# A decoder layer on one core: split products in cross-attention's output projection, bias rows in the upper part of A

## The reference, cut to what matters

```
def memory_cross_attention(hn, memn, w_xq, w_xkv, w_xo):
    ...
    s = jnp.einsum('bshd,bmhd->bhsm', q, k) * XATTN_HEAD_DIM ** -0.5
    p = jax.nn.softmax(s, axis=-1)
    o = jnp.einsum('bhsm,bmhd->bshd', p, v).reshape(B, S, D)
    return o @ w_xo                      # 256x1024 by 1024x1024

def moe_ffn(...):
    logits = xt @ w_router + b_router
    ...
    gu = xb @ w_gate_up[e] + b_gate_up[e]     # w_gate_up: 32 x 1024 x 2048
    ...
    return hmid @ w_down[e] + b_down[e]       # w_down: 32 x 1024 x 1024
```

## Time and profile before

| | us |
|---|---|
| median of 3 runs (1182.55 to 1183.7) | 1182.78 |
| the profiled execution | 1183.28 |
| its span | 1181.5 |
| PE busy | 1114.9 (94%) |
| DVE busy | 320.5 (27%) |
| ACT busy | 233.0 (20%) |
| POOL busy | 41.1 (3%) |

### The profile page before, as it was taken

How to read it: one execution, slowest core, us unless ns; L and a number is a source line. 1 busy time by engine, 2 the same in 40 slices (tenths; PEclk the granted TensorE clock), 3 DMA queues, 4 the chain that set the end, 5 groups by cost and what they waited for, 6 DMA issues and landing times.

```text
span 1181.5 us, 12743 instructions
## 1 busy us (share of the span) xinstructions
PE 1114.9 (94%) x5408; PEld 495.3 (42%) x5409; DVE 320.5 (27%) x719; ACT 233.0 (20%) x460; POOL 41.1 (3%) x41
## 2 busy tenths in 40 slices
PE   8999999999999999799999999999999999999896
PEld 7887668753333333233333333333333333333332
DVE  5787665332111112111222111111111111111112
ACT  6575665431000001000100000000000000000002
POOL 0010240220000000000000000000000000000000
PEclk9999999999999999899999999999999999999999
DMA  9915337779999999999999999999999999999995
GB/s 361 350 52 178 108 143 285 262 293 423 429 427 427 428 429 426 426 429 427 427 427 429 428 425 429 428 426 428 429 426 428 429 427 427 428 428 428 426 429 227
DMA packets 44586, 445.50 MB, mean 377 GB/s; under 512 B 6096, under 2 KB 10288, under 8 KB 19728
## 3 DMA queue, kind: packets, MB, share of 16 engines
q1 hardware_dynamic: 42784, 444.38, 90.3%
q10 hardware_dynamic: 1744, 0.28, 0.2%
HBM read 443.60 MB, written 1.05 MB: 376 GB/s over the span
## 4 chain that ended last, share of the span: by engine, by line
PE 65%; DMA 28%; DVE 4%; ACT 2%; issue 1%; SPq 0%; DVEq 0%; ACTq 0%
PE ps L2087 23%; PE ps L2096 13%; DMA R<-in_w_gate_up 12%; PE ps L1590 4%; DMA R<-in_w_down 4%; DMA XMT<-in_w_gate_up 4%; DMA MK<-in_w_gate_up 4%; PE ps L2116 4%; DMA A<-in_w_gate_up 4%; PE ps L2063 4%; PE ps L1610 3%; PE ps L1612 3%; PE ps L1611 3%; PE ps L1947 2%; PE ps L2078 2%; PE ps L1839 1%
## 5 line engine op out<-in xcount | busy, mean ns | idle before, releaser
L2087 PE MATMUL ps<-R,convT 128*64 128x512 f32 x1104 | 246.2, 593 | 14.3 <-DMA R<-in_w_gate_up 14.3
L1488 DVE TENSOR_SCALAR A<-ps 128x512 f32<-128x512 f32 x30 | 20.7, 692 | 645.8 <-PE ps L2087 645.8
L2087 PEld LDWEIGHTS ps<-R,convT 128*64 128x64 f32 x1104 | 76.8, 137 | 169.9 <-issue 137.2
L2096 PE MATMUL ps<-R,A 128*64 128x512 f32 x592 | 131.9, 593 | 1.3 <-DMA R<-in_w_down 1.2
L956 ACT ACTIVATE A<-A 128x512 f32<-128x512 f32 x30 | 18.9, 630 | 471.7 <-DVE A L1488 471.7
L2096 PEld LDWEIGHTS ps<-R,A 128*64 128x64 f32 x592 | 41.4, 137 | 78.8 <-issue 75.1
L2116 PE MATMUL ps<-A,convT 64*128 64x512 f32 x248 | 61.6, 615 | 2.1 <-ACT A L963 1.4
L963 ACT COPY A<-ps 128x512 f32<-128x512 f32 x30 | 17.6, 585 | 221.3 <-PE ps L2096 221.3
L2063 PE MATMUL ps<-H,convT 128*64 128x512 f32 x256 | 60.4, 592 | 0.1
L2078 PE MATMUL ps<-A,convT 96*64 96x512 bf16 x192 | 33.0, 393 | 20.6 <-ACT A L961 13.7
L2087 PE MATMUL ps<-XMT,convT 128*64 128x512 f32 x208 | 46.9, 593 | 2.0 <-DMA XMT<-in_w_gate_up 2.0
(11 more groups left out here) (323 smaller groups left out, 1287.9 us busy)
## 6 DMA issues: line engine op xcount, KB each, us to landing
R<-in_w_gate_up SPq DMA_DIRECT2D x69, 2048.0 KB, 35.3
R<-in_w_down SPq DMA_DIRECT2D x37, 2048.0 KB, 39.7
...
```

Of the source, the lines that this page charges most:

```text
L1488: V.tensor_scalar(gcl, bank(G_BANK), LIM, None, ALU.min).then_inc(m_gcl, 1)
L2087: last = mm(bank(b)[s * SLOTS:(s + 1) * SLOTS, :], xg[:, 4 * (j % 2) + 2 * c + j // 2, :], w[:, c * 2 * FF + at + s * BANK:c * 2 * FF + at ...
L2096: last = mm(bank(o)[s * SLOTS:(s + 1) * SLOTS, :], h[:, c, i * SLOTS:(i + 1) * SLOTS], w[:, c * D + s * BANK:c * D + (s + 1) * BANK], star ...
```

## The change

The output projection is made of split products. Its units are 16 more of the same kind (`UNITS_O`): raw weights in R as before, low parts in their place, high parts in tile QK, eight at a time, so that the second eight wait for the block (1,0) that last reads the first eight. The output's own high and low parts take XMT (`o_hi`, `o_lo`). The blocks' order becomes first half of (0,0), transposes, rest of (0,0), then (1,0), (0,1), (1,1), with the router's transposes inside (1,1). QK and A change places in the ring: fill 4 goes to A, fill 7 to QK. Fill 4 has no wait of its own any more, 6 waits for block (1,0), 7 for the last block, 8 and 9 for nothing more. The raw biases stand in A's columns 5632 to 7680 and in convT, and POOL alone splits them (`bias_parts`), at once when they land. The router's rows move from XMT to A's upper part (`h2T`), where they wait for the biases (`pool_bias`). Two counters of POOL become one (`pool_mix`).

```diff
--- before.py
+++ after.py
@@ -194,6 +196,8 @@
             return (R_p if base is R else A_p)[:, at:at + BANK]
 
         def high(u):
+            if u >= UNITS_O:
+                return QK_p[:, u % KC * BANK:(u % KC + 1) * BANK]
             if u >= UNITS:
                 at = (12288, 4096)[u // KC - 7] + u % KC * BANK
                 return R_p[:, at:at + BANK]
...
+        o_hi = XMT_p[:, 2048:4096].rearrange("p (t c n) -> p t c n", t=T, c=KC)
+        o_lo = XMT_p[:, 0:2048].rearrange("p (t c n) -> p t c n", t=T, c=KC)
         h_hi = XMT_p[:, 0:2048].rearrange("p (k n) -> p k n", k=KC)
         h_lo = XMT_p[:, 2048:4096].rearrange("p (k n) -> p k n", k=KC)
         sq_junk = [QK[:, 2048 + t * D:2048 + (t + 1) * D] for t in range(T)]
         P2T = xtf.rearrange("p (t h m n) -> p t h m n", t=T, h=XH, m=2)
 
         R_slot = [R[:, f * 4096:(f + 1) * 4096] for f in range(6)]
...
+        ring = [R_slot[0], R_slot[2], R_slot[1], R_slot[3], A[:, 0:4096], XM[:, :], R_slot[4], QK[:, :], R_slot[5], XMT[:, :],
                 MK[:, MOE_KEEP:MOE_KEEP + 4096]]
 
 
         BW = 2 * FF + D
-        b_raw = A[0:96, 0:BW]
+        b_raw = [A[0:96, 5632:5632 + 2 * FF], convT[0:96].rearrange("p c n -> p (c n)")]
         b_prt = A[0:96, 4096:4096 + BW // 2].bitcast(BF16)
         gcl, ucl, sgm, hmf, orow = (A[:, 5632 + 512 * i:6144 + 512 * i] for i in range(5))
         hTm = hmf.rearrange("p (c n) -> p c n", c=4)
         hT_b, selT_b, orow_b = sgm.rearrange("p (c n) -> p c n", c=4), gcl[:, 0:S], hmf
         junk = [A[:, 6144:7168], A[:, 6144:7168]]
+        h2T = A[:, 5632:7680].rearrange("p (k n) -> p k n", k=KC)
+        h2_junk = A[:, 7680:8192].bitcast(BF16)
         early_junk = convT[:].rearrange("p c n -> p (c n)")
 
         cvf = convT[:].rearrange("p c n -> p (c n)")
...
@@ -514,21 +521,15 @@
                             sp.wait_ge(g_done, 1)
                     if n == 2:
                         sp.wait_ge(pe_two, TWO["q", 1])
-                        for part in range(3):
-                            sp.dma_start(b_raw[part * E:(part + 1) * E, 0:2 * FF], b_gate_up[0]).then_inc(ld_bias, 16)
-                            sp.dma_start(b_raw[part * E:(part + 1) * E, 2 * FF:BW], b_down[0]).then_inc(ld_bias, 16)
-                    if n == 4:
-                        sp.wait_ge(pe_s2, T)
+                        for i, src in enumerate((b_gate_up, b_down)):
+                            for part in range(3):
+                                sp.dma_start(b_raw[i][part * E:(part + 1) * E, :], src[0]).then_inc(ld_bias[i], 16)
                     if n == 5:
                         sp.wait_ge(pe_two, TWO["oT", 1])
                     if n == 6:
+                        sp.wait_ge(pe_unit, UNITS + KC)
+                    if n == 7:
                         sp.wait_ge(pe_xo, 3)
-                    if n == 7:
-                        sp.wait_ge(act_part, 3)
-                    if n == 8:
-                        sp.wait_ge(pe_xo, 4)
-                    if n == 9:
-                        sp.wait_ge(pe_lg, T)
                     if n == 10:
                         sp.wait_ge(pe_cnt, T + 1)
                         sp.wait_ge(m_bsel, 1)
...
@@ -594,11 +595,18 @@
                     pool.wait_ge(act_osq, t + 1)
                     fold_squares(sq[:, t:t + 1])
 
-                def bias_rest(n):
-                    pool.wait_ge(act_part, 3 - n)
-                    link(nc.gpsimd.tensor_tensor(b_raw[0:n * E], b_raw[0:n * E], b_prt[0:n * E], ALU.subtract), pool_res)
-
-                bias_rest(2)
+                def bias_parts(i):
+
+                    raw = b_raw[i]
+                    prt = b_prt[:, 2 * FF * i:2 * FF * i + raw.shape[1]]
+                    pool.wait_ge(ld_bias[i], 16 * 3)
+                    link(nc.gpsimd.tensor_copy(prt, raw))
+                    for n in (2, 1):
+                        link(nc.gpsimd.tensor_tensor(raw[0:n * E], raw[0:n * E], prt[0:n * E], ALU.subtract))
+                        link(nc.gpsimd.tensor_copy(prt[0:n * E], raw[0:n * E]), pool_bias)
+
+                bias_parts(0)
+                bias_parts(1)
                 pool.wait_ge(pe_two, TWO["pv", 1])
                 link(nc.gpsimd.iota(iot.rearrange("p (s n) -> p s n", s=2), pattern=[[0, 2], [1, SLOTS]], base=0,
                                     channel_multiplier=0, allow_small_or_imprecise_dtypes=True), pool_moe)
...
+                    else:
+                        act.wait_ge(ld_o2, 32)
+                        act.wait_ge(pe_s2, T)
                     if 4 <= u < UNITS:
                         act.wait_ge(pe_unit, slot_free(u))
-                    if u >= UNITS:
+                    if u >= UNITS_O + KC:
+                        act.wait_ge(pe_unit, UNITS + kc + 1)
+                    if UNITS <= u < UNITS_O:
                         nc.scalar.activation(high(u), raw(u), ACT.Copy, scale=prm[:, R_XA + kc:R_XA + kc + 1]).then_inc(act_uhi, 1)
                     else:
                         nc.scalar.copy(high(u), raw(u)).then_inc(act_uhi, 1)
...
                 exps2(1)
                 pv_second(0)
                 second("pT", 1, 5, P2T[:, 1, 2:4].rearrange("p h m n -> p (h m n)"))
-                second("oT", 0, 1, last_half(oT2, 0))
-                act.wait_ge(ld_bias, 16 * 6)
-                nc.scalar.copy(b_prt, b_raw).then_inc(act_part, 1)
+                split_high("oT", 0, o_hi[:, 0])
+                for u in range(UNITS_O + 4, UNITS_O + 6):
+                    unit_high(u)
                 pv_second(1)
-                second("oT", 1, 5, last_half(oT2, 1))
-                for n in (2, 1):
-                    act.wait_ge(pool_res, 3 - n)
-                    nc.scalar.copy(b_prt[0:n * E], b_raw[0:n * E]).then_inc(act_part, 1)
+                for u in range(UNITS_O + 6, UNITS_O + 8):
+                    unit_high(u)
+                split_high("oT", 1, o_hi[:, 1])
+                for u in range(UNITS_O + 8, UNITS_O + 16):
+                    unit_high(u)
+                act.wait_ge(pool_bias, 4)
                 for t in range(T):
-                    act.wait_ge(dve_h2, 2 * t + 2)
-                    act.wait_ge(pe_two, TWO["oT", t])
-                    root(t, H[:, t, :], junk[t]).then_inc(act_rt, 1)
+                    act.wait_ge(dve_h2, 3 + t)
+                    root(t, H[:, t, :], h2_junk).then_inc(act_rt, 1)
                     if t == 0:
                         second_gain("h2T", t, R_MOE)
                 for t in range(T):
...
 
                 first("pT", 0, 0, P2T[:, 0, 0:2].rearrange("p h m n -> p (h m n)"))
                 max2(1)
+                for u in range(UNITS_O, UNITS_O + 3):
+                    unit_low(u)
                 pv_first(0)
                 first("pT", 1, 4, P2T[:, 1, 0:2].rearrange("p h m n -> p (h m n)"))
-                first("oT", 0, 0, first_half(oT2, 0))
+                unit_low(UNITS_O + 3)
+                split_low("oT", 0, o_hi[:, 0], o_lo[:, 0])
                 pv_first(1)
-                first("oT", 1, 4, first_half(oT2, 1))
+                for u in range(UNITS_O + 4, UNITS_O + 6):
+                    unit_low(u)
+                split_low("oT", 1, o_hi[:, 1], o_lo[:, 1])
+                for u in range(UNITS_O + 6, UNITS_O + 8):
...
+                        dve.wait_ge(pe_unit, UNITS + KC)
+                    else:
+                        dve.wait_ge(pe_xo, 1 + t + n)
                     hn = H[:, t, n * BANK:(n + 1) * BANK]
                     link(V.tensor_tensor(hn, hn, bank(4 * t + 2 + n), ALU.add), dve_h2)
 
@@ -1942,16 +1973,17 @@
                                         high(u), low(u), c)
                     return last
 
-                def half_rows(t, n, lhs, w, chunks=range(KC)):
+                def half_rows(t, n, chunks=range(KC)):
                     for c in chunks:
-                        last = mm(bank(4 * t + 2 + n), lhs(c), w(c, n), start=(c == 0), stop=(c == KC - 1))
+                        u = UNITS_O + n * KC + c
+                        if c % 4 == 0:
+                            pe.wait_ge(dve_sp, SPLIT["oT", t] + c // 4 + 1)
+                        if t == 0:
+                            pe.wait_ge(dve_ulo, u + 1)
+                        last = split_mm(bank(4 * t + 2 + n), o_hi[:, t, c, :], o_lo[:, t, c, :], high(u), low(u), c)
+                        if (t, n) == (1, 0):
+                            last.then_inc(pe_unit, 1)
                     return last
-
-                def wo(c, n):
-                    return w_o2[:, n, c, :]
-
-                def ot(t):
-                    return lambda c: oT2[:, t, c, :]
 
                 pe.wait_ge(dve_h1, T + 1)
                 eight_transposes("h1T", 0, H[:, 0, :])
...
                 ready("pv", 1)
                 eight_transposes("oT", 1, XS[:, 1, :])
-                half_rows(0, 1, ot(0), wo).then_inc(pe_xo, 1)
-                ready("oT", 1)
-                half_rows(1, 0, ot(1), wo).then_inc(pe_xo, 1)
```

(53 more changed lines are left out.)

28 lines of the change are left out of this document (13 added, 15 removed).

## The result

The changed kernel took 1193.03 us (median of 4, 1191.43 to 1193.99) against 1183.09 for the kernel before (4 runs): ratio 1.0079, 95% interval 1.0067 to 1.0090. Timed a second time, side by side, it took 1192.27 (5 runs) against 1183.59 (15): 1.0078, interval 1.0065 to 1.0092. The profiled execution of the changed kernel is the shortest of its first four, 1191.43 us with a span of 1189.4. It is 8.15 us longer than the profiled execution of before, and its span 7.9. The numbers of lines moved: the low part is line 1059, the scaling of the maxima 1381, the weighted values 1408, POOL's cast, subtraction and cast 603, 605 and 606, the fills 507.

What follows compares the result with a forecast made beforehand. The end was taken as the moment the weight stream becomes unbroken, set by fill 7. Waits for POOL 9.5 us, less 0.8 for products, plus 1.5 for clock, gave +10.2: 1193.5 profiled, 1193.0 median, range 1183.5 to 1203.

Steps and rivals of the forecast that it cites:

- The end is fill 7 plus a constant: Weight stream: gapless once fill 7 is in, 6.7 us after its issue, so the change counts only through that moment.
- The products by themselves: Output projection on PE: split chunks 0.70 us against 0.86, 5.1 us less PE work, but only 0.8 us gained overall.
- The wait of chunk 6: Block (0,0) on PE: chunk 6 waits 1.3 us for a low part behind the output's own low parts on DVE.
- POOL's prices: Bias splitting on POOL: casts 1.9 and 1.06 us, subtractions 4.0 and 2.0, 20.9 in sum, from 213.1 to 234 us.
- dear casts: Rival: POOL's casts at its two-input price, work 33 us, waits 17, time 1201.3 us; chance 0.13 with middling casts.
- A low part waits out POOL's running instruction: DVE beside POOL: each low part, with two SBUF inputs, is blocked until POOL's running instruction ends; low parts of 2 to 5 us.
- no block: Rival: POOL blocks neither low parts nor scalings on DVE, low parts stay 0.69 us, time 1182.0 us; chance 0.14.
- only scalings: Rival: POOL blocks only DVE's scalings, exponentials 1.65 then 2 us late, time 1183.9 us; chance 0.05.
- The waits, 9.2 us before the weighted values: DVE's scalings and low parts wait for POOL, so tile 0's weighted values come at 230.5 us in place of 221.34.
- My chain: DVE's order, one instruction per POOL instruction: first scaling behind the first cast, then second scaling and three low parts each wait.
- PE's clock, 1.5 us: PE after its 7.1 us pause: granted clock falls to 0.50 and work slows by 1.5 us, between 0 and 2.4.
- Sum: Fill 7 in at 270.1 us for 259.85: +10.2, from 9.5 waits, less 0.8, plus 1.5; profiled execution 1193.5, median 1193.0.

Runs made afterwards that it cites:

- e_nopool: Changed kernel without POOL's subtractions and the casts behind them, its first casts issued after all sixteen low parts; 1183.58 us, ratio 0.9998 to the kernel before.
- e_writes: Changed kernel with POOL's ten instructions on the biases replaced by fourteen memsets, which only write; 1183.82 us, ratio 1.0003 to the kernel before.
- e_small: Changed kernel with POOL's bias work in pieces of 512 columns, 30 instructions in place of ten; 1187.07 us, ratio 1.0029 to the kernel before.
- e_warm: Changed kernel with 26 idle products on PE before the transposes of the first weighted values; 1189.77 us, ratio 1.0054 to the kernel before.

## Why the prediction was right, point by point

- **The end is fill 7 plus a constant.** Right, and shown eleven times, 927.6 to 928.2 us.
- **The products by themselves, 0.8 us gained at most.** Right. e_nopool has 252.61 for a forecast of 252.4 and is within 0.2% of before; its profiled execution is 0.74 us shorter than that of before. The wait of chunk 6 was 1.20 us (1.3).
- **POOL's prices.** Right: casts 1.89 and 1.03 us (1.9 and 1.06), subtractions 4.07 and 2.12 (4.0 and 2.0), first cast at 213.20 (213.1). POOL ended at 236.5, and not at 234: of the 2.4 us more it worked, 1.6 are its own waits for DVE, since the block works both ways. For dear casts the sum was wrong: by the prices given they make 30.6 us, an end near 244, and not 33 and 248. Nothing hung on it.
- **A low part waits out POOL's running instruction.** Right, by e_nopool, e_writes and e_small. The rivals "no block" and "only scalings" fall: three low parts took 7.45 us. The row that spoke for "no block", the DVE instruction at 174.74 that was not lengthened beside POOL, stays unexplained.
- **The waits, 9.2 us before the weighted values.** Mis-sized: 5.85. My chain began one instruction too early, with the first scaling behind the first cast (1.65 us). It slipped in ahead in all three profiles, by 0.14, 0.46 and 0.16 us; landings of these loads spread from 3.4 to 5.3 us, so the chain could not tell which of the two comes first. So DVE was one place ahead, the first low part was free, and two waited where I had three. The weighted values came at 226.88 for 230, and fills 5, 6 and 7 at 238.89, 248.75 and 261.26 for 240, 249 and 263.
- **PE's clock, 1.5 us.** 2.8 in the first profile, 1.4 in the other two; e_warm bears out the mechanism.
- **Sum.** Forecast +10.2 us for the profiled execution, measured +8.15: in the scale of the table 48.20 - 39.27 = 8.9 over the path without POOL, of which 5.85 are waits, 2.8 clock and 0.3 other. So the waits were 3.35 us too dear and the clock 1.3 too cheap, and the forecast for the profiled execution, 1193.5, was 2.1 too high. That the median hit all the same, 1193.03 for 1193.0, is luck: I took the profiled execution to be 0.5 us above the median, as before, and it was 1.6 below it. In the second comparison the loss is 8.7 us. What makes the other executions longer stays open. The kernel before spreads over 2.0 us in that comparison, the changed kernel over 2.9, and e_warm over 0.8 in five executions: that points to the slow clock for a part of it, and does not show it.
